# A hybrid decoder trunk in which 17 of 22 FFN column blocks use a seven-product scheme: other buffers, other summing and another order for its weight combinations

## The chip, the cores and the metric

The kernel runs on one core of one Trainium2 chip. Times are device microseconds of one execution; the median of three executions is compared. Matmul operands are fp32 values split in two fp32r parts, a rounded "high" one and the "low" rest, so that each product of a 128x128 weight block with 260 activation columns takes three matmuls (high x high, high x low, low x high).

## The reference, cut to what matters

```
for l in range(2):                                  # 512 prompt tokens and 8 sample tokens
    m = mixer(rmsnorm(h, w_mix_pre))                # gated DeltaNet and retention heads, one input, one output projection
    h = h + rmsnorm(m, w_mix_post)
    x = rmsnorm(h, w_ffn_pre)
    gate, up = split(x @ w_gate_up)                 # 1024 -> 2 x 2816
    h = h + rmsnorm((silu(gate) * up) @ w_down, w_ffn_post)
```

The change is in the product x @ w_gate_up and in silu(gate) * up; everything else is the same in both kernels.

## The kernel before, in words

The activations lie transposed: hT has 8 blocks of 128 model rows, and the 520 tokens as two halves of 260 columns. A layer is a long run of matmuls on TensorE (PE). Weights arrive as 512 KB slabs in two stage buffers (SP issues them, line 481), ScalarE (ACT) rounds each to Wh (line 1313) and VectorE (DVE) takes the rest Wl (line 1865), three slabs deep.

The gate and up matrices have 22 column blocks each. The first NP = 5 pairs are computed directly, as 10 tiles of 48 matmuls (the first three tiles by halves in `first_halves`, line 687, the other seven at line 681). DVE takes gate tile i = 2j out of PSUM (line 2461) and up tile i = 2j+1 (line 2479), each with the norm's factor `rb`; PE's tile i waits until tile i-2 has been taken out. Between these two instructions DVE also runs `x_scaled`, `x_sum` and `x_low`, which make the seven combinations of activations (tile XU), and ACT runs `weighted` (line 1709) and `x_high` for them.

The other Q = 17 pairs q go by a Strassen-Winograd scheme, `strassen(q)` (lines 1234 to 1236): the 2x2 blocks are gate and up (rows) by upper and lower half of the model dimension, and by the two token halves. Seven products UA11, US2, US1, UA12, US3, US4, UA22, in this order, of 12 matmuls each, replace eight. Their weights are quarters of the block column, QW = 512 columns wide each: those of UA11, UA12 and US4 are single quarters; US1 and US3 are sums of two quarters, US2 of three, UA22 of four. The seven outputs go to three PSUM banks (a, b, c), so that US3 and UA22 both accumulate on b after US2. Even and odd q use different banks (4, 5, 6 and 0, 1, 2), and three sets of buffers hold full, high and low weights: C for q = 0, B for odd, A for even q.

What makes the weights of pair q before: SP loads quarter (0,0) twice with one 512 KB transfer (line 503, semaphore b11), quarter (1,1) twice with another (line 508) and quarter (0,1) (line 509). POOL then adds quarter (1,0) to one copy of each by two accumulating DMAs (lines 659 and 663, t1 and t3), which wait for the plain loads. DVE adds US2 (line 2403) and UA22 (line 2412). ACT rounds blocks two by two (`w_high`, line 1732), DVE takes the rests (`w_low`, line 2420). The loads for q go into the set that q-2 used, so line 503 waits until product US1 of q-2 is done, line 508 until US4 is.

What takes the products out: ACT copies the first (`first_copy`, p1, line 1739); DVE runs five `post` instructions per q: U2 (line 2430), TD (2432), C22 (2435), C12 (2437), C21 (2439); ACT does two SiLU halves (lines 1745, 1749); DVE multiplies (`gated`, line 2446). PE's US3 waits for post U2, US4 for TD, UA22 for C22. Each engine runs its list in program order: DVE's order per q is C21 of q-1, the last `w_low` of q, `gated`, then the sums and rests of q+1 between the posts of q. After the 17 pairs comes the down projection (lines 681 and 687), for which the state buffers dst (loaded and stored by POOL) also serve a decode update.

Of the kernel before, what the change touches and what calls it, by code (L numbers as in the profile page):

```python
# [8 lines left out]
def trunk(nc, xT, w_slabs, w_ba, w_rows, dt_bias, a_log, conv_hist, state_gdn, state_ret, c_f32, c_rope,  # L9
# [7 lines left out]
    P = 128  # L17
    KT = 8
# [47 lines left out]
    U2, TD, C22, C12, C21 = range(1, POSTS + 1)  # L66
    P1_COPY, C11_SILU, C21_SILU, HALVES = 1, 2, 3, 3
    W_T2, W_T4, W_LO, W_STEPS = 1, 2, 3, 6
# [30 lines left out]
    with ctx:  # L99
# [142 lines left out]
        tdif = at("tdif", A0, XU_N + (FT - 2) * HF, [P, HC])  # L242
# [13 lines left out]
        pu = at("pu", UP0, 0, [P, 2, HC])  # L256
        p1, u2 = pu[:, 0], pu[:, 1]
# [42 lines left out]
        def acc_banks(q):  # L300
            return (0, 1, 2) if q % 2 else (4, 5, 6)
# [80 lines left out]
        def heads_of(i):  # L382
# [23 lines left out]
            "b11_loaded b2_loaded t1_summed t3_summed p_done post_done ffn_rest ffn_round gate_half "  # L406
# [69 lines left out]
        def _(sp):  # L476
# [14 lines left out]
            def quarters(l, q):  # L491

                N = l * Q + q
                w = w_set(q)[2]
                if q == 0:
                    sp.wait_ge(s["state_stored"], (l + 1) * 32)
                elif q < 3:
                    sp.wait_ge(s["tile_done"], l * TILES + T_DN)
                else:
                    sp.wait_ge(s["p_done"], (N - 2) * UN + US1 + 1)  # L500
                if N:
                    sp.wait_ge(s["b11_loaded"], N * 16)
                sp.dma_start(w[:, UA11:US1 + 1:2], quarter(l, q, 0, 0).unsqueeze(1).to_broadcast([P, 2, QW])).then_inc(s["b11_loaded"], 16)
                if q >= 3:
                    sp.wait_ge(s["p_done"], (N - 2) * UN + US4 + 1)
                if N:
                    sp.wait_ge(s["b2_loaded"], N * 32)
                sp.dma_start(w[:, US3:US4 + 1], quarter(l, q, 1, 1).unsqueeze(1).to_broadcast([P, 2, QW])).then_inc(s["b2_loaded"], 16)
                sp.dma_start(w[:, UA12], quarter(l, q, 0, 1)).then_inc(s["b2_loaded"], 16)
# [65 lines left out]
        def _(pool):  # L575
# [13 lines left out]
            for l in range(DEPTH):  # L589
# [59 lines left out]
                pool.wait_ge(s["dr_mm"], (l + 1) * 16)  # L649
                load_state(l, 0, False)  # L650
                load_state(l, 1, False)
                for q in range(Q):

                    N = l * Q + q
                    w = w_set(q)[2]
                    if N:
                        pool.wait_ge(s["t1_summed"], N * 16)
                    pool.wait_ge(s["b11_loaded"], (N + 1) * 16)
                    pool.dma_start(w[:, US1], quarter(l, q, 1, 0), accum_op=ALU.add).then_inc(s["t1_summed"], 16)
                    if N:  # L660
                        pool.wait_ge(s["t3_summed"], N * 16)
                    pool.wait_ge(s["b2_loaded"], (N + 1) * 32)
                    pool.dma_start(w[:, US3], quarter(l, q, 1, 0), accum_op=ALU.add).then_inc(s["t3_summed"], 16)
# [11 lines left out]
        def _(pe):  # L675
# [53 lines left out]
            for l in range(DEPTH):  # L729
# [474 lines left out]
                def strassen(q):  # L1204
# [3 lines left out]
                    a_, b_, c_ = acc_banks(q)  # L1208
                    for u, bank in enumerate((a_, b_, c_, a_, b_, c_, b_)):
                        if q == 0:  # L1210
                            pe.wait_ge(s["ffn_rest"], l * REST + 8 + u + 1)
                        if u % 2 == 0:
                            pe.wait_ge(s["ffn_rest"], l * REST + X_STEPS + q * W_STEPS + W_LO + u // 2)
                        if u == UA11:
                            if q == 0:
# [6 lines left out]
                        elif u == US2 and q >= 2:  # L1222
                            pe.wait_ge(s["post_done"], (N - 2) * POSTS + C21)
                        elif u == UA12:
                            pe.wait_ge(s["gate_half"], N * HALVES + P1_COPY)
                        elif u == US3:
                            pe.wait_ge(s["post_done"], N * POSTS + U2)
                        elif u == US4:
                            pe.wait_ge(s["post_done"], N * POSTS + TD)
                        elif u == UA22:  # L1230
                            pe.wait_ge(s["post_done"], N * POSTS + C22)
                        for k in range(4):
                            cols = slice(k * P, (k + 1) * P)
                            mm(PS[:, bank, 0:HC], hi_[:, u, cols], XU[:, u, 0, k], start=k == 0 and u < 3, stop=False, skip_group_check=True)  # L1234
# [63 lines left out]
        def _(act):  # L1298
# [16 lines left out]
            for l in range(DEPTH):  # L1315
# [399 lines left out]
                def w_high(q, c):  # L1715
# [3 lines left out]
                    us = slice(2 * c, min(2 * c + 2, UN))  # L1719
                    if c == 0:  # L1720
                        act.wait_ge(s["b11_loaded"], (N + 1) * 16)
                        act.wait_ge(s["ffn_rest"], l * REST + X_STEPS + q * W_STEPS + W_T2)
                    elif c == 1:
                        act.wait_ge(s["t1_summed"], (N + 1) * 16)
                        act.wait_ge(s["b2_loaded"], (N + 1) * 32)
                    elif c == 2:
                        act.wait_ge(s["t3_summed"], (N + 1) * 16)
                    else:
                        act.wait_ge(s["ffn_rest"], l * REST + X_STEPS + q * W_STEPS + W_T4)
                    if q >= 3:  # L1730
                        act.wait_ge(s["p_done"], (N - 2) * UN + us.stop)
# [978 lines left out]
```

## Time and profile before

| what | value |
| --- | --- |
| median of 3 runs | 1453.88 us (1452.79 to 1454.06) |
| the profiled execution's own time | 1450.49 us |
| its span, first to last instruction | 1448.7 us |
| mean granted TensorE clock | 0.988 |
| first layer's seven-product stage | 392.5 to 587.2 us |
| second layer's | 1110.2 to 1305.8 us |

The span is what the trace's rows cover; the profiled execution's own time has 1.8 us more around it. Rows are in microseconds from the span's start. A matmul's row lasts 0.28 us but the next one starts 0.12 us after it, since they overlap: so the time between starts is what counts.

### The profile page before, as it was taken

The numbers are of one execution on the slowest core, as the hardware profiler recorded it, in microseconds if no ns is written. First come the engines' busy times: TensorE is split into PE (matmuls) and PEld (weight loads), VectorE is DVE, ScalarE is ACT, GpSimd is POOL, SyncE is SP. The second block draws the span as 40 slices with busy tenths as digits, with TensorE's granted clock in tenths as the row PEclk, the third lists the DMA queues.
The fourth block names the chain that finished last, engine by engine and source line by source line (L and its number), as shares of the span: only waits on it lengthen the run. The fifth ranks groups of instructions, "written<-read, shape, count | busy, mean of one in ns | idle before, by whom it ended". The sixth has DMA issues, their size and how long they took to land.

```text
span 1448.7 us, 29260 instructions
## 1 busy us (share of the span) xinstructions
PE 1386.1 (96%) x12172; PEld 1354.6 (94%) x12172; DVE 997.2 (69%) x1641; ACT 626.7 (43%) x1196; POOL 159.7 (11%) x209
## 2 busy tenths in 40 slices
PE   9999999998989999999999999999988989999997
PEld 8999999998988989999999999999988889999997
DVE  7745896877666767854586568877766666677544
ACT  5135464465433434522442364643753444354222
POOL 0001211100011111011000011210001111110110
PEclk9999999999999999999999999999999999999998
DMA  5331341131466675355313322421224566653552
GB/s 200 117 102 60 96 131 62 62 105 59 119 144 158 164 162 150 120 178 180 122 59 117 103 68 86 118 75 63 91 90 126 128 159 174 156 140 129 179 183 77
DMA packets 81092, 174.20 MB, mean 120 GB/s; under 512 B 20673, under 2 KB 24129, under 8 KB 80961
## 3 DMA queue, kind: packets, MB, share of 16 engines
q1 hardware_dynamic: 63344, 128.81, 28.1%
q0 software_dynamic: 17616, 43.53, 12.7%
q8 instruction: 96, 1.57, 0.4%
q14 instruction: 36, 0.29, 0.1%
HBM read 159.53 MB, written 12.78 MB: 119 GB/s over the span
## 4 chain that ended last, share of the span: by engine, by line
PE 71%; DMA 12%; DVE 11%; issue 3%; ACT 2%; SPq 1%; DVEq 0%; ACTq 0%; POOLq 0%
PE PS L681 46%; DMA fullB<-w_slabs 8%; PE PS L687 4%; PE PS L1234 4%; PE PS L1236 3%; PE PS L1235 3%; DMA fullA<-w_slabs 3%; DVE loB L2420 1%; DVE Wl L1865 1%; DVE hT L1903 1%; DVE Xl L1882 1%; DVE mT L1902 1%; DVE loA L2420 1%; PE PS L875 1%; DVE conv L1992 1%
## 5 line engine op out<-in xcount | busy, mean ns | idle before, releaser
L681 PE MATMUL PS<-Xh,Wh 128*128 128x260 f32 x1376 | 287.7, 290 | 11.6 <-DVE sqb L2479 9.3
L1313 ACT ACTIVATE Wh<-stage 128x1024 fp32r<-128x1024 f32 x143 | 151.1, 1058 | 339.5 <-PE PS L681 322.6
L681 PE MATMUL PS<-Xh,Wl 128*128 128x260 f32 x1376 | 278.6, 284 | 0.0
L681 PE MATMUL PS<-Xl,Wh 128*128 128x260 f32 x1376 | 278.2, 284 | 0.0
L1865 DVE TENSOR_TENSOR Wl<-stage,Wh 128x1024 fp32r<-128x1024 f32 x143 | 174.6, 1222 | 103.8 <-ACT Wh L1313 103.2
L681 PEld LDWEIGHTS PS<-Xh,Wh 128*128 128x128 f32 x1376 | 213.8, 191 | 15.6 <-issue 11.0
L681 PEld LDWEIGHTS PS<-Xl,Wh 128*128 128x128 f32 x1376 | 213.6, 190 | 0.0
L681 PEld LDWEIGHTS PS<-Xh,Wl 128*128 128x128 f32 x1376 | 213.5, 190 | 0.0
L1234 PE MATMUL PS<-XU,hiA 128*128 128x260 f32 x448 | 128.9, 288 | 14.4 <-DVE pu L2430 7.4
L1234 PE MATMUL PS<-XU,hiB 128*128 128x260 f32 x448 | 128.5, 287 | 10.0 <-DVE pu L2430 4.8
L1236 PE MATMUL PS<-XU,loA 128*128 128x260 f32 x448 | 126.9, 283 | 0.0
L1236 PE MATMUL PS<-XU,loB 128*128 128x260 f32 x448 | 126.9, 283 | 0.0
L1235 PE MATMUL PS<-XU,hiB 128*128 128x260 f32 x448 | 126.5, 282 | 0.0
L1235 PE MATMUL PS<-XU,hiA 128*128 128x260 f32 x448 | 126.5, 282 | 0.0
L681 PE MATMUL PS<-actH,Wh 128*128 128x260 f32 x616 | 124.0, 282 | 0.0
L681 PE MATMUL PS<-actH,Wl 128*128 128x260 f32 x616 | 123.9, 282 | 0.0
L681 PE MATMUL PS<-actL,Wh 128*128 128x260 f32 x616 | 123.9, 282 | 0.0
L1234 PEld LDWEIGHTS PS<-XU,hiA 128*128 128x128 f32 x448 | 84.3, 188 | 18.9 <-DVE fullB L2403 8.4
L681 PEld LDWEIGHTS PS<-actH,Wh 128*128 128x128 f32 x616 | 97.2, 188 | 1.4
L1234 PEld LDWEIGHTS PS<-XU,hiB 128*128 128x128 f32 x448 | 84.3, 188 | 13.5 <-DVE fullA L2403 5.8
L1732 ACT ACTIVATE hiB<-fullB 128x1024 fp32r<-128x1024 f32 x64 | 57.4, 945 | 87.9 <-DMA fullB<-w_slabs 33.2
L681 PEld LDWEIGHTS PS<-actL,Wh 128*128 128x128 f32 x616 | 94.8, 188 | 0.0
(380 smaller groups left out, 2916.5 us busy)
## 6 DMA issues: line engine op xcount, KB each, us to landing
stage<-w_slabs SPq DMA_DIRECT2D x143, 512.0 KB, 3.4
fullB<-w_slabs SPq DMA_DIRECT2D x32, 512.0 KB, 4.5
fullA<-w_slabs SPq DMA_DIRECT2D x32, 512.0 KB, 4.7
dst<-state_ret POOLq DMA_DIRECT2D x32, 256.0 KB, 3.7
dst<-state_gdn POOLq DMA_DIRECT2D x32, 256.0 KB, 4.1
fullB<-w_slabs POOLq DMA_DIRECT2D x32, 256.0 KB, 5.8
fullA<-w_slabs POOLq DMA_DIRECT2D x32, 256.0 KB, 5.1
fullB<-w_slabs SPq DMA_DIRECT2D x16, 256.0 KB, 5.4
```

Source lines behind the costliest of these rows:

```text
L681: ins = mm(pj(slot)[:, a], w[:, ws, pos, :], x[:, a, :], start=first and w is Wh and x is xh, stop=last and w is Wl)
L687: ins = mm(pj(slot)[:, a], w[:, ws, pos, :], x[:, a, :], start=first and w is Wh and x is xh, stop=last and w is Wl)
L875: ins = mm(PS[rows, 7, B_U:B_U + P], vectors, dst[:, u % 2, j, :], start=n == 0, stop=n == 7 and u < 8, skip_group_check=True)
L1234: mm(PS[:, bank, 0:HC], hi_[:, u, cols], XU[:, u, 0, k], start=k == 0 and u < 3, stop=False, skip_group_check=True)
L1235: mm(PS[:, bank, 0:HC], hi_[:, u, cols], XU[:, u, 1, k], start=False, stop=False, skip_group_check=True)
L1236: ins = mm(PS[:, bank, 0:HC], lo_[:, u, cols], XU[:, u, 0, k], start=False, stop=k == 3, skip_group_check=True)
L1313: A(Wh[:, G % NW], stage[:, G % NS], ACT.Copy).then_inc(s["hi_split"], 1)
L1732: A(hi_[:, us], full[:, us], ACT.Copy).then_inc(s["ffn_round"], 1)
L1865: V.tensor_tensor(Wl[:, G % NW], stage[:, G % NS], Wh[:, G % NW].bitcast(fp32), ALU.subtract).then_inc(s["lo_split"], 1)
L1882: V.scalar_tensor_tensor(Xl[:, k, a], hT[:, k, a], prm[:, layer, row:row + 1], Xh[:, k, a].bitcast(fp32), ALU.mult, ALU.subtract).then_inc ...
L1902: step(V.tensor_tensor(src, src, rb[:, a:a + 1].to_broadcast([P, k1 - k0, HC]), ALU.mult))
L2420: V.tensor_tensor(lo_[:, us], full[:, us], plain(hi_[:, us]), ALU.subtract).then_inc(s["ffn_rest"], 1)
```

## The change

Quarter blocks are loaded once each into buffers of their own (raw1 holds two, raw12, raw21) and SP starts the load for the next pair when DVE has read the buffer. POOL adds nothing any more; DVE makes US1 and US3 with one instruction. The seventh product gets a fourth PSUM bank, the fifth is added in place, the third is copied by ACT (m5). The order of work on ACT and DVE is rewritten: DVE makes nearly all weights of q+1 during q, and around the direct tiles ACT's `weighted` and DVE's `x_scaled`, `x_sum` and `x_low` come behind the instructions that empty PSUM. p1 and u2 lie in rb, m5 where tdif was.

```diff
-    U2, TD, C22, C12, C21 = range(1, POSTS + 1)
+    U2, U3, C22, C12, C21 = range(1, POSTS + 1)
@@
+        p1, u2 = rb[:, 0], rb[:, 1]
+        raw1 = at("raw1", RP0, 0, [P, 2, QW])
+        raw12 = at("raw12", UP0, 0, [P, QW])
+        raw21 = at("raw21", W0, 2 * UN * QW, [P, QW])
@@ acc_banks
-            return (0, 1, 2) if q % 2 else (4, 5, 6)
+            return (0, 1, 2, 3) if q % 2 else (4, 5, 6, 7)
@@ quarters (SP)
+                    sp.wait_ge(s["ffn_rest"], used + W_T13)
+                sp.dma_start(raw12[:], quarter(l, q, 1, 0)).then_inc(s["b12_loaded"], 16)
...
+                    sp.wait_ge(s["ffn_rest"], used + W_LO05)
+                sp.dma_start(raw1[:, 0], quarter(l, q, 0, 0)).then_inc(s["b1_loaded"], 16)
+                sp.dma_start(raw1[:, 1], quarter(l, q, 1, 1)).then_inc(s["b1_loaded"], 16)
...
+                    sp.wait_ge(s["ffn_rest"], used + W_LO3)
+                sp.dma_start(raw21[:], quarter(l, q, 0, 1)).then_inc(s["b21_loaded"], 16)
@@ POOL
+                pool.wait_ge(s["ffn_rest"], l * REST + X_STEPS + (Q - 1) * W_STEPS + W_LO05)
                 load_state(l, 0, False)
                 load_state(l, 1, False)
-                for q in range(Q):
...
-                    pool.dma_start(w[:, US1], quarter(l, q, 1, 0), accum_op=ALU.add).then_inc(s["t1_summed"], 16)
...
-                    pool.dma_start(w[:, US3], quarter(l, q, 1, 0), accum_op=ALU.add).then_inc(s["t3_summed"], 16)
@@ strassen (PE)
-                    for u, bank in enumerate((a_, b_, c_, a_, b_, c_, b_)):
+                    for u, bank in enumerate((a_, b_, c_, a_, b_, c_, d_)):
...
+                            pe.wait_ge(s["ffn_rest"], l * REST + X_STEPS + q * W_STEPS + W_LO12)
...
                         elif u == US3:
+                            pe.wait_ge(s["ffn_rest"], l * REST + X_STEPS + q * W_STEPS + W_LO46)
                             pe.wait_ge(s["post_done"], N * POSTS + U2)
                         elif u == US4:
-                            pe.wait_ge(s["post_done"], N * POSTS + TD)
-                        elif u == UA22:
-                            pe.wait_ge(s["post_done"], N * POSTS + C22)
+                            pe.wait_ge(s["gate_half"], N * HALVES + M5_COPY)
+                        elif u == UA22 and q >= 2:
+                            pe.wait_ge(s["post_done"], (N - 2) * POSTS + C21)
@@ ACT
                 for j in range(NP):
...
-                    if j == 0:
-                        for k in range(KT):
-                            weighted(k)
                     act.wait_ge(s["tile_free0"], (T0 + T_GU + 2 * j) // 2 + 1)
                     A(gp, gp, ACT.Silu).then_inc(s["gate_silu"], 1)
                     if 2 * j + 1 + NW < 2 * NP:
                         hi(G0 + S_GU + 2 * j + 1 + NW)
+                    if j < 2:
+                        for k in range(4 * j, 4 * j + 4):
+                            weighted(k)
...
                     if q:
                         gate_second(q - 1)
+                    if q + 1 < Q:
+                        w_high(q + 1, W_HI05)
                     first_copy(q)
                     if q + 1 < Q:
-                        w_high(q + 1, 0)
-                        w_high(q + 1, 1)
+                        w_high(q + 1, W_HI3)
+                        w_high(q + 1, W_HI12)
+                        fifth_copy(q)
+                        w_high(q + 1, W_HI46)
                         gate_first(q)
-                        w_high(q + 1, 2)
-                        w_high(q + 1, 3)
@@ DVE, new and changed steps
+                    V.tensor_tensor(full[:, US1:US3 + 1:2], raw1[:], raw12[:].unsqueeze(1).to_broadcast([P, 2, QW]), ALU.add).then_inc(s["ffn_rest"], 1)
...
+                    V.tensor_tensor(full[:, US2], full[:, US1], raw1[:, 1], ALU.add).then_inc(s["ffn_rest"], 1)
...
+                    elif n == U3:
+                        dve.wait_ge(s["post_done"], N * POSTS + U2)
+                        ins = V.tensor_tensor(p1, PS[:, b_, 0:HC], p1, ALU.add)
                     elif n == C22:
+                        dve.wait_ge(s["gate_half"], N * HALVES + M5_COPY)
+                        dve.wait_ge(s["post_done"], N * POSTS + U3)
+                        ins = V.tensor_tensor(up[:, 1], m5[:], p1, ALU.subtract)
@@ DVE, direct tiles: gate tile taken out, then
-                    if j == 0:
-                        x_scaled(0)
-                    elif j == 1:
+                    if j == 1:
+                        x_scaled(2)
                         x_scaled(3)
-                        x_sum(0)
...
+                    elif j == 4:
+                        w_sums13(0)
                         w_sum2(0)
-                        w_sum4(0)
+                        w_low(0, W_HI05)
@@ up tile taken out, product, then
                     if j == 0:
+                        x_scaled(0)
                         x_scaled(1)
-                        x_scaled(2)
...
+                    elif j == 4:
+                        w_sum4(0)
+                        w_low(0, W_HI3)
+                        w_low(0, W_HI12)
+                        w_low(0, W_HI46)
@@ DVE, the order per q
                     if q:
                         post(q - 1, C21)
+                    if q + 1 < Q:
+                        w_sums13(q + 1)
+                        w_sum2(q + 1)
+                        w_low(q + 1, W_HI05)
+                        if q:
+                            gated(q - 1)
+                        post(q, U2)
+                        w_sum4(q + 1)
+                        w_low(q + 1, W_HI3)
+                        w_low(q + 1, W_HI12)
+                        post(q, U3)
+                        post(q, C22)
+                        w_low(q + 1, W_HI46)
+                        post(q, C12)
```

HI05, HI3, HI12 and HI46 name the products (by their number 0 to 6 in the order above) whose weights one instruction rounds, W_LO05 and so on those whose rest is taken; T13, T2 and T4 are the sums for US1 and US3, for US2 and for UA22.

## Rows read from the trace of the kernel before

**Rows 1.** Stretch: length, busy (count) of PE, PEld, DVE, ACT, POOL, clock, DMA share, GB/s

```profile
392.00:588.00 196.00, 181.34 (x1435) 177.30 (x1436) 135.66 (x206) 81.07 (x121) 27.90 (x32) 0.98 0.64 158
```

**Rows 2.** PE in short stretches: length, busy (count), granted clock, DMA share, GB/s

```profile
347.20:352.20 5.00, 4.99 (x25) 0.55 0.13 32
1065.50:1070.50 5.00, 4.96 (x30) 0.70 0.15 32
392.50:397.50 5.00, 4.99 (x29) 0.66 0.85 273
1110.10:1115.10 5.00, 4.94 (x23) 0.50 0.86 261
605.00:615.00 10.00, 10.00 (x84) 1.00 0.37 133
```

**Rows 3.** Timeline of PE: first seven-product matmul and first down matmul, both layers

```profile
392.51 0.41 PE L1234 MATMUL PS<-XU,hiC 128*128 128x260 f32 x1 [2.71 <-DVE loC L2420]
...
587.17 0.41 PE L681 MATMUL PS<-actH,Wh 128*128 128x260 f32 x2
...
1110.16 0.56 PE L1234 MATMUL PS<-XU,hiC 128*128 128x260 f32 x1 [2.71 <-DVE loC L2420]
...
1305.83 0.41 PE L681 MATMUL PS<-actH,Wh 128*128 128x260 f32 x2
```

**Rows 4.** What ended PE's idle time before line 1234 (us, times)

```profile
  DVE pu L2430: 16.3, 16
...
  DVE sqb L2435: 10.9, 24
```

**Rows 5.** Chain that ended last, within one pair of the first layer

```profile
525.51 3.87 DMA fullB<-w_slabs
...
529.90 6.77 DMA fullB<-w_slabs
```

**Rows 6.** Timeline of DVE in one pair: start, duration

```profile
532.44 1.23 DVE L2420 TENSOR_TENSOR loA<-fullA,hiA 128x1024 fp32r<-128x1024 f32 x1 [1.96 <-ACT hiA L1732]
533.58 0.42 DVE L2437 TENSOR_TENSOR sqb<-PS,pu 128x260 f32<-128x260 f32 x1
...
534.26 0.68 DVE L2420 TENSOR_TENSOR loA<-fullA,hiA 128x512 fp32r<-128x512 f32 x1
534.86 0.69 DVE L2446 TENSOR_TENSOR actF<-sqb 128x520 f32<-128x520 f32 x1
```

**Rows 7.** Timeline of DVE: two sums, the second waiting for the first

```profile
384.69 0.68 DVE L2403 TENSOR_TENSOR fullC<-fullC 128x512 f32<-128x512 f32 x1
385.41 0.69 DVE L2412 TENSOR_TENSOR fullC<-fullC 128x512 f32<-128x512 f32 x1
```

**Rows 8.** DMA issues: KB each, median us from issue to landing

```profile
fullA<-w_slabs SPq DMA_DIRECT2D x16, 256.0 KB, 5.9
...
dst<-state_ret POOLq DMA_DIRECT2D x32, 256.0 KB, 3.7
...
rope<-c_rope SPq DMA_DIRECT2D x1, 520.0 KB, 8.3
```

**Rows 9.** Timelines of PE, ACT and DVE before the fourth direct tile, first layer

```profile
342.27 0.28 PE L687 MATMUL PS<-Xh,Wl 128*128 128x260 f32 x1
347.21 0.77 PE L681 MATMUL PS<-Xh,Wh 128*128 128x260 f32 x2 [4.67 <-DVE sqb L2479]
...
342.60 5.06 ACT L1709 ACTIVATE XF<-hT,prm 128x520 f32<-128x520 f32 x8
347.56 0.62 ACT L1765 ACTIVATE sqb<-sqb 128x520 f32<-128x520 f32 x1
348.09 1.04 ACT L1313 ACTIVATE Wh<-stage 128x1024 fp32r<-128x1024 f32 x1
...
341.32 0.70 DVE L2461 TENSOR_TENSOR sqb<-PS,rb 128x520 f32<-128x520 f32 x1 [0.61 <-ACT rb L1355]
345.21 1.24 DVE L2381 TENSOR_TENSOR XF<-XF,rb 128x1040 f32<-128x1040 f32 x1 [3.20 <-ACT XF L1709]
```

More of the change, by code:

```diff
@@ L1222, in strassen @@
                         elif u == US2 and q >= 2:
-                            pe.wait_ge(s["post_done"], (N - 2) * POSTS + C21)
+                            pe.wait_ge(s["post_done"], (N - 2) * POSTS + U3)
+                        elif u == US1 and q >= 2:
+                            pe.wait_ge(s["post_done"], (N - 2) * POSTS + C12)
                         elif u == UA12:
@@ L1718, in w_high @@
                     lo_, hi_, full = w_set(q)
[L1719 to L1727, printed above, removed]
-                    else:
-                        act.wait_ge(s["ffn_rest"], l * REST + X_STEPS + q * W_STEPS + W_T4)
-                    if q >= 3:
-                        act.wait_ge(s["p_done"], (N - 2) * UN + us.stop)
-                    A(hi_[:, us], full[:, us], ACT.Copy).then_inc(s["ffn_round"], 1)
+                    rest = l * REST + X_STEPS + q * W_STEPS
+                    if c == W_HI05:
+                        act.wait_ge(s["b1_loaded"], (N + 1) * 32)
+                        to, src = hi_[:, UA11:US4 + 1:US4], raw1[:]
+                    elif c == W_HI3:
+                        act.wait_ge(s["b21_loaded"], (N + 1) * 16)
+                        to, src = hi_[:, UA12], raw21[:]
+                    elif c == W_HI12:
+                        act.wait_ge(s["ffn_rest"], rest + W_T2)
+                        to, src = hi_[:, US2:US1 + 1], full[:, US2:US1 + 1]
+                    else:
+                        act.wait_ge(s["ffn_rest"], rest + W_T4)
+                        to, src = hi_[:, US3:UA22 + 1:2], full[:, US3:UA22 + 1:2]
+                    A(to, src, ACT.Copy).then_inc(s["ffn_round"], 1)
                 def first_copy(q):
@@ L2411, in w_sum4 @@
                     dve.wait_ge(s["ffn_rest"], l * REST + X_STEPS + q * W_STEPS + W_T2)
-                    V.tensor_tensor(w[:, UA22], w[:, US2], w[:, UA12], ALU.add).then_inc(s["ffn_rest"], 1)
+                    V.tensor_tensor(full[:, UA22], full[:, US2], raw21[:], ALU.add).then_inc(s["ffn_rest"], 1)
                 def w_low(q, c):
                     lo_, hi_, full = w_set(q)
-                    us = slice(2 * c, min(2 * c + 2, UN))
-                    if c == 0:
+                    if c == W_HI05:
+                        us, src = slice(UA11, US4 + 1, US4), raw1[:]
+                    elif c == W_HI3:
+                        us, src = UA12, raw21[:]
+                    else:
+                        us = slice(US2, US1 + 1) if c == W_HI12 else slice(US3, UA22 + 1, 2)
+                        src = full[:, us]
@@ L2424, in post @@
                     N = l * Q + q
-                    a_, b_, c_ = acc_banks(q)
-                    part = {U2: US2, TD: US1, C22: US3, C12: US4, C21: UA22}[n]
-                    dve.wait_ge(s["p_done"], N * UN + part + 1)
+                    a_, b_, c_, d_ = acc_banks(q)
+                    if n != C22:
+                        dve.wait_ge(s["p_done"], N * UN + {U2: US2, U3: US3, C12: US4, C21: UA22}[n] + 1)
                     if n == U2:
@@ L2508, in _ @@
                         gated(q - 1)
-                    if not last:
-                        w_sum2(q + 1)
-                    else:
                         rest_act(0, 2)
-                    post(q, U2)
-                    if not last:
-                        w_sum4(q + 1)
-                    else:
+                        post(q, U2)
                         rest_act(2, 2)
-                    post(q, TD)
-                    if not last:
-                        w_low(q + 1, 0)
-                        w_low(q + 1, 1)
-                    else:
@@ L2523, in _ @@
                         lo(G0 + S_DN)
                         rest_act(4, 2)
-                    post(q, C22)
-                    if not last:
-                        w_low(q + 1, 2)
-                    else:
+                        post(q, U3)
+                        post(q, C22)
                         rest_act(6, 2)
-                    post(q, C12)
+                        post(q, C12)
                 lo(G0 + S_DN + 1)
```

111 lines of the change are left out of this document (46 added, 65 removed).

## The prediction

> **What bounds the kernel now.** I first read the busy times of the seven-product stretch [rows 1]. PE is busy for 181.34 of 196.00 us, VectorE for 135.66, ScalarE for 81.07. PE is the bound, yet it has holes. In the down projection, without holes and at full clock, 10 us hold 84 matmuls [rows 2], so one matmul costs 0.12 us. A pair q is 7 x 12 = 84 matmuls, 10.08 us, and 17 pairs are 1428 x 0.12 = 171.36 us.
>
> The PE timeline [rows 3] gives what the stage takes: 587.17 - 392.51 = 194.66 us in the first layer and 1305.83 - 1110.16 = 195.67 in the second. The excess is 23.30 and 24.31 us, 47.6 together; one pair takes (194.66 + 195.67) / 34 = 11.48 us, not 10.08.
>
> The waits say who makes the holes [rows 4]: 16.3 us on post U2 (line 2430, before US3) and 10.9 us on post C22 (line 2435, before UA22). VectorE isn't out of time, so something holds it. The chain through one pair [rows 5] names it: a plain load of 3.87 us, then an accumulating one, started from POOL, of 6.77 us. They stand in series, 10.6 us, and VectorE's sums and rests come behind: that loop can't turn in 10.08 us. VectorE's instruction before the posts was itself idle for 1.96 us [rows 6].
>
> A second loss lies ahead of the stage [rows 9]. The third tile's last matmul starts at 342.27, the fourth tile's first at 347.21: 4.94 us instead of 0.12. PE waits for line 2479, which stands behind `x_scaled(0)` (345.21), and that waited 3.20 us for ScalarE's eight `weighted` (342.60, 5.06 us).
>
> **The change, part by part.**
>
> *Direct tiles.* The up tile's evacuation no longer has `x_scaled(0)` ahead of it. The gate tile's starts at 341.32; at the step of 0.61 that such a pair of instructions has (0.70 less 0.09) it starts at 341.93, ends at 342.62, and PE goes on 0.15 later (before: 345.21 + 1.15 + 0.70 + 0.15 = 347.21), at 342.77. The hole falls from 4.94 to 0.50: 4.44 saved per layer, 8.9 in all.
>
> The clock goes with it. After the hole, 5 us hold 25 matmuls in the first layer and 30 in the second, at granted clocks of 0.55 and 0.70, against 41.7 at full clock [rows 2]: 16.7 x 0.12 = 2.0 and 11.7 x 0.12 = 1.4 us, 3.4 in all. A hole of 0.5 us won't do this; those of about 1.3 us within the stage [rows 4] are followed by full pace.
>
> What moved comes back as new waits. ScalarE loads a table until 342.60, SiLU takes 0.53 and a slab's rounding about 1.0 [rows 9]; four `weighted` at 0.63 then end at 346.7. `x_scaled(0)` and `(1)` take 2.3 (1.15 each) and stand ahead of the third tile's gate evacuation, 349.05 to 349.74, so the fifth tile starts at 349.89. PE is done with the fourth at 342.77 + 5.76 = 348.53: a wait of 1.36. The same again: SiLU and a rounding from 349.78, four `weighted` until 353.9, two `x_scaled`, evacuation until 356.9, start at 357.04, while PE was ready at 355.65: 1.39. After these the evacuations come in time. Cost 2.75 per layer, 5.5 in all; the bounds are 0 (if PE's queue covers it) and 4 per layer.
>
> *Handover to the first pair.* Before, PE sat idle for 2.71 us for evacuation, product and one rest [rows 3]. Now `w_sum4` and the short rest of HI3 come in too, 0.60 each [rows 6], before the rest PE waits for: 1.2 more per layer, 2.4 in all. The first loads don't matter: they are issued as soon as the slabs' queue allows, over 15 us ahead, though raw21 has to wait for the eighth direct tile.
>
> *The stage itself.* Time R is a pair's first matmul. I take VectorE's steps from start to start [rows 6]: a two-block instruction 1.14 (533.58 - 532.44), two posts 0.68 (534.26 - 533.58), so 0.34 each, a one-block one 0.60, `gated` 0.61. An instruction that waits for the one before it steps by 0.72 rather than 0.60 [rows 7]. Per pair there are five posts (1.70), three rests of two blocks and `w_sums13` (4.56), `w_sum2`, `w_sum4` and the one-block rest (1.80), `gated` (0.61), and two such waits (0.24): 8.9 us, under 10.08. Added against before is `w_sums13`, 1.14, in place of both POOL sums.
>
> In order: C21 of q-1 starts at R+0.20, `w_sums13` 0.55, `w_sum2` 1.81, a rest 2.43, `gated` 3.58, U2 4.19 (done 4.6), `w_sum4` 4.54, rests 5.14 and 5.74, then U3. PE wants U2 at R+5.76: 1.1 to spare. U3 needs US3, done at about R+7.36, so VectorE waits until 7.40; U3, C22, a rest and C12 end at 9.75. C21 comes at R+10.28: 0.5 to spare. UA22 has a bank of its own and no longer waits for this pair's posts. US4 needs m5, which ScalarE copies at R+4.6, wanted at 7.20. ScalarE has eight instructions, none longer than 1.06: at most 8.5 us. The holes at US3 and UA22 go.
>
> *Loads.* Each is single-buffered, so its loop has to turn within a pair. raw1 is the tightest: `w_sums13`, `w_sum2` and the rest take 1.26 + 0.60 + 1.22 = 3.1, the second issue and semaphores about 0.5, then the landing. A quarter landed in 5.9 us behind a 512 KB transfer and a state block of its size in 3.7 [rows 8]. That makes 7.3 to 9.5, under 10.08; I take the lower half, since each pair loads 1.05 MB instead of 1.8 MB of plain and accumulating traffic (the stretch moved 158 GB/s [rows 1]). POOL's two first state loads now wait for the last pair's raw1; their reader comes in the down projection, ten and more us later: nothing. At the last pair, `fifth_copy` stands ahead of a slab's rounding, 0.4 us with 3 to spare: nothing.
>
> *Left of the excess.* The clock after the handover. The first 5 us held 29 matmuls in the first layer and 23 in the second [rows 2], 12.7 x 0.12 = 1.5 and 18.7 x 0.12 = 2.2. The idle time grows, and the second layer wasn't yet at full clock: I take 2.1 per layer, 4.2, with bounds 3.0 and 7.
>
> **Sum:** -8.9 - 3.4 + 5.5 + 2.4 - 47.6 + 4.2 = -47.8 us. The profiled execution took 1450.49, so 1402.7; the median of the runs is 3.4 us above it, which gives **1406 us**. Bounds of the single terms: -55 (no new waits, short clock losses) to -43 (4 us of waits per layer, 7 of clock), so 1399 to 1411. A measurement of this kernel tells 0.2%, 2.9 us, from nothing.
>
> **The rivals.**
>
> *VectorE becomes the bound.* For: 8.9 us of 10.08 rest on instructions starting up to 0.09 us before the one ahead ends. If thirteen of them with their semaphores each ended first, they would take 9.73 us in full durations plus 13 x 0.04: 10.25 per pair, 0.17 over PE. 34 x 0.17 = 5.8 us, so 1412. Against: the early starts are between instructions that have semaphore waits now [rows 6]. The Trainium skill ("VectorE: DVE Perf Modes", section "The DRAIN you can't avoid") says that the next instruction does not start until the pipeline is empty; by that rule the sum would be this rival's. The row at 533.58 shows a start every 0.34 us for 0.42 us posts, so here the trace bears it out only for dependent ones.
>
> *Loads come late, in part.* The raw1 loop needs a landing under 6.5 us. At 6.9 a pair takes 10.5, 34 x 0.42 = 14 us more: 1420. For: three more loads share SP's queue, each issue holding it; against: less traffic. This also covers the case that the new waits in the direct tiles grow.
>
> *Slower than before.* The place is the same loop, `w_sums13` ahead of all posts: single buffers put load, sums and rest in series, which the old kernel had spread over two sets. From a landing of 8.0 us on, the pair takes over 11.6 us and eats the 4.5 us gained outside. 8.3 us was seen once, for a table load with many others in flight [rows 8]: (3.6 + 8.3 - 11.48) x 34 - 4.5 = +10, 1464. Against it speaks every other row. The Trainium skill ("DMA: Bandwidth & Descriptors", section "Measured (HBM→SBUF, 128 partitions, SWDGE, issued from GpSimd)") tells to batch transfers to at least 1 MiB; its rule speaks against cutting 512 KB transfers into quarters, and by it this loop would be slower than a joint load. The state block's row, a quarter MB in 3.7 us, shows no such penalty.
>
> *It doesn't do what it says:* the posts stay late because ScalarE's rounding of raw1 holds `first_copy`, now behind it. It would move US3's hole to UA12, some 0.5 us a pair: 1423. The order gives 1.9 us to spare.
>
> **How the numbers follow.** My forecast 0.72, VectorE bound 0.12, loads partly late or ScalarE late 0.12 together, slower 0.03, 0.01 for an exact balance. The range takes the forecast's bounds and the second and third case's times: 1400 to 1420. Faster 0.96, same 0.01, slower 0.03.
>
> **What would show it.** Right: the seven-product stage is 173 to 175 us in each layer; no POOL transfers of weights; gaps before US3 and UA22 under 0.1 us; pairs start every 10.1 us; C21 starts 0.2 us after PE ends the pair, with VectorE idle before it. In the direct tiles a hole of 0.5 us before the fourth tile and two new ones of 1.4. Wrong: VectorE never idle and PE waiting for a rest or for U2; `w_sums13` waiting for raw1; landings over 6 us; a hole over 5 us at the handover.

## The result, and the profile after

The changed kernel took 1403.72 us (median of 4 runs, 1401.79 to 1404.53) against 1453.34 us (4 runs): ratio 0.9665, 95% interval 0.9638 to 0.9693. The prediction was 1406. Run again on another occasion it took 1403.68 us, ratio 0.9665 (0.9647 to 0.9683). The profiled execution took 1401.79 us with a span of 1400.0, where the sum had 1402.7 for it. The sum was added up for the profiled execution, and 3.4 us were put on it for the median; in the changed kernel the median lies 1.9 us above the profiled execution.

The two stretches of seven products, and PE in short stretches; columns as in [rows 1] and [rows 2]:

```profile
388.00:561.00 173.00, 172.74 (x1426) 172.77 (x1427) 151.83 (x218) 84.49 (x138) 1.11 (x2) 0.99 0.30 106
1083.00:1256.00 173.00, 172.61 (x1425) 172.64 (x1426) 151.76 (x218) 84.41 (x138) 1.11 (x2) 0.99 0.30 106
```

```profile
341.00:346.00 5.00, 4.90 (x41) 1.00 0.37 125
1036.10:1041.10 5.00, 4.90 (x41) 1.00 0.35 127
388.20:393.20 5.00, 4.94 (x30) 0.69 0.27 102
1083.30:1088.30 5.00, 4.91 (x28) 0.66 0.29 102
```

PE is busy all through the stage, and VectorE for 152 of 173 us where it was 136 of 196 [rows 1]. The DMA engines move 106 GB/s instead of 158. The fourth direct tile starts at full clock (41 matmuls in 5 us where [rows 2] had 25 and 30).

The PE timeline, first layer, first and last matmul of the stage and what is left of the holes around it:

```profile
341.10 0.48 PE L676 MATMUL PS<-Xh,Wh 128*128 128x260 f32 x2 [0.20 <-DVE sqb L2493]
...
348.18 0.36 PE L676 MATMUL PS<-Xh,Wh 128*128 128x260 f32 x1 [1.12 <-DVE sqb L2476]
...
355.32 0.36 PE L676 MATMUL PS<-Xh,Wh 128*128 128x260 f32 x1 [1.17 <-DVE sqb L2493]
...
388.26 0.56 PE L1231 MATMUL PS<-XU,hiC 128*128 128x260 f32 x1 [3.91 <-DVE loC L2433]
...
561.25 0.41 PE L676 MATMUL PS<-actH,Wh 128*128 128x260 f32 x2
...
579.53 0.50 PE L1197 MATMUL PS<-vblk,krows 96*128 96x512 f32 x1 [0.40 <-DVE vblk L2369]
```

The stage takes 561.25 - 388.26 = 172.99 us, in the second layer (1083.39 to 1256.45) 173.06: 44.3 us less than in [rows 3]. What ended PE's idle time before the stage's first lines has one entry left, the start of the stage itself:

```profile
its engine sat idle before it (us, times) until:
  DVE loC L2433: 16.0, 4
```

The four are PE and its weight loads, in both layers; the two entries of [rows 4] are gone. One pair on VectorE, which answers to [rows 6]:

```profile
531.20 0.43 DVE L2454 TENSOR_TENSOR sqb<-PS,rb 128x260 f32<-128x260 f32 x1 [0.44 <-PE PS L1233]
531.54 1.22 DVE L2409 TENSOR_TENSOR fullB<-raw,raw 128x1024 f32<-128x1024 f32 x1
532.79 0.69 DVE L2414 TENSOR_TENSOR fullB<-fullB,raw 128x512 f32<-128x512 f32 x1
...
535.14 0.42 DVE L2443 TENSOR_TENSOR rb<-PS,rb 128x260 f32<-128x260 f32 x1
...
536.69 1.22 DVE L2433 TENSOR_TENSOR loB<-fullB,hiB 128x1024 fp32r<-128x1024 f32 x1
538.40 0.43 DVE L2446 TENSOR_TENSOR rb<-PS,rb 128x260 f32<-128x260 f32 x1 [0.50 <-PE PS L1233]
538.94 0.43 DVE L2450 TENSOR_TENSOR sqb<-m,rb 128x260 f32<-128x260 f32 x1
...
541.28 0.43 DVE L2454 TENSOR_TENSOR sqb<-PS,rb 128x260 f32<-128x260 f32 x1 [0.44 <-PE PS L1233]
```

The pair's matmuls start at R = 531.00. C21 comes at R+0.20, U2 at R+4.14, U3 at R+7.40 after 0.50 us of waiting for PE, and the next C21 10.08 us after the first. VectorE now waits for PE twice a pair, and PE for nobody.

The loads, as in [rows 8]; all four quarters of a pair are in one row:

```profile
raw<-w_slabs SPq DMA_DIRECT2D x136, 256.0 KB, 2.6
```

**Where 48.7 us of span went.** It is read off PE's rows. From the last matmul before the hole to the stage's first, the direct tiles took 392.51 - 342.27 = 50.24 us and take 388.26 - 340.62 = 47.64, and in the second layer 49.54 and 47.68: 4.5 us. The stages give 44.3. What follows a stage got longer, by 1.0 us from the first stage's end to the second layer's hole and by 0.7 us from the second stage's end to the end: 1.7. The last 1.65 us are the start of the program: the last matmul before the first hole starts at 340.62 where it started at 342.27, and the change doesn't touch what is ahead of it. This execution had a granted clock of 1.00 in the span from 3 to 23 us (117 matmuls), the one of before 0.91 (104 matmuls). So 47.0 us are the change's, where the sum had 47.8. The repetition agrees: it had 102 matmuls at 0.91, its last matmul before the hole starts at 342.47, and its span is 46.7 us under that of before.

### The profile page after: what moved, and what is told of

Read it like the earlier page. It is cut to its first block, busy times and chain, and to the rows that moved or that the text cites. A ratio compares the mean times of both kernels' runs of the same rounds, so it can differ in the third digit from the quotient of the medians.

```text
span 1400.0 us, 29086 instructions
## 1 busy us (share of the span) xinstructions
PE 1366.9 (98%) x12172; PEld 1343.3 (96%) x12172; DVE 1040.2 (74%) x1675; ACT 634.9 (45%) x1230; POOL 100.7 (7%) x141
## 4 chain that ended last, share of the span: by engine, by line
PE 83%; DVE 10%; ACT 3%; issue 2%; DMA 1%; SPq 0%; DVEq 0%; ACTq 0%
PE PS L676 43%; PE PS L1231 8%; PE PS L1232 8%; PE PS L1233 8%; PE PS L682 5%; DVE Wl L1873 2%; DVE hT L1911 1%; ACT Wh L1310 1%; DVE Xl L1890 1%; ACT XF L1706 1%; DVE actL L2467 1%; ACT actH L1756 1%; DVE mT L1910 1%; PE PS L870 1%; PE PS L1197 1%
## 5 line engine op out<-in xcount | busy, mean ns | idle before, releaser
L676 PEld LDWEIGHTS PS<-actH,Wl 128*128 128x128 f32 x616 | 94.8, 188 | 0.0
```

The costliest lines, as they stand in the source:

```text
L676: ins = mm(pj(slot)[:, a], w[:, ws, pos, :], x[:, a, :], start=first and w is Wh and x is xh, stop=last and w is Wl)
```

## The experiments

Differences are taken from 1403.7 us, and each ratio is to the kernel before on the run's own occasion. On four occasions the kernel before took 1449.7 to 1453.3 us (medians), so differences between times of two occasions are uncertain by some 3 us. The lengths of the stages are read from the traces, two for each run.

### The transfers that add, taken out of the old kernel

```diff
-                    pool.dma_start(w[:, US1], quarter(l, q, 1, 0), accum_op=ALU.add).then_inc(s["t1_summed"], 16)
...
-                    pool.dma_start(w[:, US3], quarter(l, q, 1, 0), accum_op=ALU.add).then_inc(s["t3_summed"], 16)
@@ ACT and DVE, waits
-                        act.wait_ge(s["t1_summed"], (N + 1) * 16)
+                        act.wait_ge(s["b11_loaded"], (N + 1) * 16)
```

> The kernel before with POOL's two accumulating transfers per pair left out (quarter (1,0) is missing from the weights of US1, US3, US2 and UA22); the instructions that waited for them wait for the plain loads. Everything else is old: order, three banks, buffers. Theory (the serial pair of transfers, 3.9 and 6.8 us, is what holds the old stage): the stage falls from 195 us to about 173 to 178 a layer, 1410 to 1420. Rival (the old order on VectorE and the shared bank make most of the holes): the stage stays over 185 us, 1430 and up.

1409.83 us, ratio 0.9712 (0.9697 to 0.9726). The stage takes 174.08 and 175.33 us. Its first matmul and the first of the down projection, and PE's idle time before the stage's first line:

```profile
393.68 0.55 PE L1222 MATMUL PS<-XU,hiC 128*128 128x260 f32 x1 [2.71 <-DVE loC L2408]
...
567.76 0.41 PE L669 MATMUL PS<-actH,Wh 128*128 128x260 f32 x2
```

```profile
  DVE loC L2408: 11.2, 4
  issue: 1.3, 3
  DVE sqb L2423: 0.7, 2
```

With the old order, three banks and two buffer sets, the stage is within 1.1 and 2.3 us of the changed kernel's as soon as nobody waits for an addition by a transfer. So the accumulating transfers were the cause: 20.6 and 20.3 us of the 23.3 and 24.3. The waits in [rows 4] on posts were their effects, passed on by VectorE's list. This run takes away the wait and the traffic together: the DMA engines move 128 GB/s in the stage instead of 158, and the joint 512 KB loads land in 3.9 and 4.0 us (medians) instead of 4.7 and 4.5. How much of the gain is the lighter traffic isn't told apart, but the 0.5 to 0.8 us at the landings are small beside the accumulating transfer's 6.77 in [rows 5].

Which loop was too long can be read from the kernel before. The 3.87 and 6.77 us of [rows 5] don't come back to their own start within one pair: with two buffer sets the load of a pair waits for product US1 of two pairs earlier. One turn for set B, SP's issues and the matmul that waited in between:

```profile
525.51 0.37 SPq L503 DMA_DIRECT2D fullB<-w_slabs  x1
...
548.28 0.37 SPq L503 DMA_DIRECT2D fullB<-w_slabs  x1
```

```profile
538.60 0.36 PE L1234 MATMUL PS<-XU,hiA 128*128 128x260 f32 x1 [0.48 <-DVE pu L2430]
```

From the issue to US3's first matmul (load, addition, VectorE's US2 sum, which stands ahead of post U2) it is 13.09 us. From there to the end of US1 of the next pair, which frees the set, PE has 72 matmuls, 8.64 us. That makes 21.7 us for two pairs, for which PE alone needs 20.16; with the hole before UA22 the turn took 22.8. Without the accumulating transfer's 6.77 us it has room, as this run shows.

The kernel leaves out one quarter of the weights; putting it back costs VectorE 1.14 us a pair, and whether the old order has room for that was not tried.

### The seventh product back in bank b

```diff
-                    for u, bank in enumerate((a_, b_, c_, a_, b_, c_, d_)):
+                    for u, bank in enumerate((a_, b_, c_, a_, b_, c_, b_)):
...
+                        elif u == UA22:
+                            pe.wait_ge(s["post_done"], N * POSTS + U3)
```

> The changed kernel with the seventh product back in bank b, so that UA22 of a pair waits until U3 of the same pair has read it. Theory (VectorE reads U3 on time now, at R+7.4 to 7.8, before UA22 wants the bank at R+8.64; the bank as such is worth nothing): 1403.7 within 2, stage 173 us. Rival (the fourth bank is what took the holes before UA22 away): 0.6 us a pair, 34 x 0.6 = +20, about 1424.

1402.02 us (1400.56 to 1403.29), ratio 0.9676 (0.9656 to 0.9695), beside 0.9665 for the changed kernel; the stage takes 173.62 and 173.58. U3 is read in time here too:

```profile
540.20 0.43 DVE L2446 TENSOR_TENSOR rb<-PS,rb 128x260 f32<-128x260 f32 x1 [0.50 <-PE PS L1233]
```

The stages are 0.6 and 0.5 us longer than the changed kernel's 172.99 and 173.06, the time isn't. The fourth bank is worth nothing that can be measured. The holes before UA22 went because U3 (and C22, which it took the bank from) come on time. Only in the last pair, where U3 stands behind a rest, PE waits 0.25 us for it, in both layers.

### The old order around the direct tiles

```diff
+                    if j == 0:
+                        for k in range(KT):
+                            weighted(k)
                     act.wait_ge(s["tile_free0"], (T0 + T_GU + 2 * j) // 2 + 1)
                     A(gp, gp, ACT.Silu).then_inc(s["gate_silu"], 1)
...
+                    if j == 0:
+                        x_scaled(0)
                     done(t + 1)
                     freed(V.tensor_tensor(up, pj(1), rb[:], ALU.mult), t + 1)
```

> The changed kernel with the old order around the ten direct tiles (all eight weighted before the first SiLU, x_scaled(0) ahead of the first up tile's evacuation, and so on); the seven-product part stays new. Theory (the new order there is worth what the prediction summed): a hole of 4.7 to 4.9 us and its slow clock come back before the fourth direct tile, the two waits of 1.3 us go, 4.4 + 1.7 - 2.6 = 3.5 us per layer, +7 us against the changed kernel: about 1410.5. The stage of the seven products stays at 173 us. Rival (the activations' order is hidden or gives back all it takes): within 2 us of 1403.7.

1412.41 us, ratio 0.9747 (0.9727 to 0.9766): 8.7 us above the changed kernel by the times, 12 by the ratios, expected 7. The hole before the fourth tile is back (4.67 us idle), the two waits are gone, and 5 us hold 25 matmuls again in the first layer and 23 in the second. The way from the hole to the stage is 3.7 and 4.0 us longer, as expected within 0.5. The stage too takes 174.14 and 174.32, 1.2 us more, and that sits in its first 5 us:

```profile
393.00:398.00 5.00, 4.98 (x23) 0.50 0.30 98
1092.30:1097.30 5.00, 4.94 (x23) 0.50 0.33 105
```

The idle time before it is the same 3.91 us as in the changed kernel, and still 23 matmuls got through instead of 30 and 28. That needn't be the old order's doing. The changed kernel's own repetition has the same 3.91 us, 29 matmuls behind it in the first layer and 22 in the second:

```profile
1084.30:1089.30 5.00, 4.90 (x22) 0.50 0.32 106
```

Its stages take 173.04 and 174.04 us. So 7.7 us are shown to be the old order's. The other 2.4, of the two stages, aren't: the changed kernel's own second stage differs by 1.0 from one execution to the next.

### VectorE's spare time: one and two more instructions per pair

```diff
+                    for _ in range(again):          # 1 or 2, for the rest of HI05 alone
+                        step(V.tensor_tensor(lo_[:, us], src, plain(hi_[:, us]), ALU.subtract))
```

> The changed kernel with one more 128x1024 instruction on VectorE per pair (the rest of HI05 taken once more into the same place), ahead of post U2; it steps by 1.26 us. Theory (VectorE needs 8.9 of 10.08 us per pair): U2 comes at about R+5.8 instead of 4.6 where PE wants it at 5.76, so 0.1 to 0.2 us a pair, +3 to +7 us: 1407 to 1411. Rival (VectorE needs 9.7 or more): 0.9 us a pair and more, +29, 1430 and up.

1412.58 us, ratio 0.9725 (0.9709 to 0.9741), +8.9: over the theory's 7, far under the rival's 29. With one more instruction PE waits for U2, and VectorE for PE only 0.16 us a pair. Rows of VectorE (the pair from `w_sums13` to `w_sums13`) and of PE (the pair's first matmul and US3's first):

```profile
487.33 0.42 DVE L2454 TENSOR_TENSOR sqb<-PS,rb 128x260 f32<-128x260 f32 x1
487.83 0.43 DVE L2456 TENSOR_TENSOR sqb<-PS,rb 128x260 f32<-128x260 f32 x1
488.18 1.22 DVE L2409 TENSOR_TENSOR fullA<-raw,raw 128x1024 f32<-128x1024 f32 x1
...
493.04 0.42 DVE L2445 TENSOR_TENSOR rb<-PS,rb 128x260 f32<-128x260 f32 x1
...
498.58 1.22 DVE L2409 TENSOR_TENSOR fullB<-raw,raw 128x1024 f32<-128x1024 f32 x1
```

```profile
487.63 0.29 PE L1231 MATMUL PS<-XU,hiB 128*128 128x260 f32 x1
...
493.61 0.36 PE L1231 MATMUL PS<-XU,hiB 128*128 128x260 f32 x1
```

The pair takes 10.40 us, 0.32 more than 10.08, with an instruction more that steps by 1.25. So U2 had 0.93 us to spare in the changed kernel (the prediction had 1.1). The loop goes through both engines: C21 (487.83) waits for PE's end of the pair, VectorE's list leads to U2 (493.04), PE's US3 waits for U2 (493.61), and PE ends the pair. C21 needs nothing of the post ahead of it, yet it steps by 0.50 instead of 0.34, and it starts 0.20 us after the next pair's first matmul as in the changed kernel: those 0.16 us are a wait for PE. VectorE's own list is therefore 10.40 - 1.25 - 0.16 = 8.99 us in the changed kernel, against 8.9 predicted and 9.7 in the rival.

> The same with two more such instructions, 2.52 us. Theory: VectorE is now the bound, 8.9 + 2.5 = 11.4 us a pair, 1.4 us over the changed kernel's on 32 pairs: +43, about 1447, back at the kernel before. Rival (9.7 or more of work): 12.2 us a pair, +68, 1470.

1450.92 us, ratio 1.0001 (0.9992 to 1.001): expected 1447. Pairs take 11.57 and 11.62 us on average, those in the middle 11.66 (US3's first matmul at 432.69 and 444.35), 1.26 more than with one added instruction. PE now waits 1.3 us a pair for U2. Two superfluous instructions a pair eat up the whole gain.

### raw1 loaded 3.3 us later in each pair

```diff
-                    sp.wait_ge(s["ffn_rest"], used + W_LO05)
+                    sp.wait_ge(s["ffn_rest"], used + W_LO12)
                 sp.dma_start(raw1[:, 0], quarter(l, q, 0, 0)).then_inc(s["b1_loaded"], 16)
```

> The changed kernel with the two raw1 loads issued 3.3 us later in each pair, after the rest of HI12 instead of the rest of HI05. Theory (a quarter lands in 2.6 us, so the loop of 6.4 + 0.5 + 2.6 = 9.5 us still turns within a pair): within 2 us of 1403.7. Rival (the loads land close to when VectorE wants them, as the 5.9 us of the old rows would have it: 12.8 us a pair): +85, about 1489.

1415.49 us, ratio 0.9753 (0.9738 to 0.9767), +11.8: neither case. One turn of the loop, SP's issues and VectorE's first sum:

```profile
491.76 0.33 SPq L508 DMA_DIRECT2D raw<-w_slabs  x1
492.13 0.43 SPq L509 DMA_DIRECT2D raw<-w_slabs  x1
```

```profile
485.37 1.22 DVE L2409 TENSOR_TENSOR fullA<-raw,raw 128x1024 f32<-128x1024 f32 x1 [1.09 <-DMA raw<-w_slabs]
...
495.77 1.23 DVE L2409 TENSOR_TENSOR fullB<-raw,raw 128x1024 f32<-128x1024 f32 x1 [1.18 <-DMA raw<-w_slabs]
```

The loop turns in 10.40 us: 6.39 from the sum to the issue, 0.37 to the second issue, then 3.64 from there to the sum. Three loads now go out within 0.9 us and their median landing is 3.4 us, not 2.6. So this loop is real, and the theory missed by its landing. In the changed kernel the second issue comes 3.47 us after the sum (535.01 after 531.54), and with a landing of 2.6 us the loop needs some 6.3 us of 10.08, an estimate from these rows.

### The handover and the direct tiles, repaired

The first run moves `w_sum4` and two rests of the first pair ahead of the last up tile's evacuation, and lets PE start with the rest of HI05 alone:

```diff
+                        if u == US2:
+                            pe.wait_ge(s["ffn_rest"], l * REST + X_STEPS + q * W_STEPS + W_LO12)
                         if u == UA11:
-                            pe.wait_ge(s["ffn_rest"], l * REST + X_STEPS + q * W_STEPS + W_LO12)
+                            pe.wait_ge(s["ffn_rest"], l * REST + X_STEPS + q * W_STEPS + W_LO05)
...
                         w_low(0, W_HI05)
+                        w_sum4(0)
+                        w_low(0, W_HI3)
+                        w_low(0, W_HI12)
                     done(t + 1)
```

> The changed kernel with w_sum4, the rest of HI3 and the rest of HI12 of the first pair put ahead of the last up tile's evacuation, and PE's wait for the rest of HI12 moved from the first product to the second. Theory (the 3.9 us hole at the handover is VectorE's order alone, and the slow clock behind it is the hole's): hole under 0.5 us, no slow clock, (3.7 + 1.6) x 2 = -10.6, about 1393. Rival (the clock falls in any case when the first pair starts, or PE waits at the second product instead): half of it or less, 1398 and up.

1391.52 us, ratio 0.9604 (0.9584 to 0.9623), -12.2. There is no hole and no slow clock, in the second layer (44 matmuls at 1.00) as in the first:

```profile
385.60:390.60 5.00, 5.00 (x44) 1.00 0.35 119
```

The stage takes 172.22 and 172.21 us, with 0.67 us of waiting for U2 of the first pair, which is late next. So its slow start was the hole's. The rows give 4.0 us for the hole and 0.8 for the stage in each layer, 9.7 in all; the other 2.5 of the 12.2 are within what two occasions differ by.

The second moves `x_scaled`, `x_sum` and the first `x_low` one evacuation on:

```diff
                     if j == 1:
-                        x_scaled(2)
-                        x_scaled(3)
+                        x_scaled(0)
+                        x_scaled(1)
...
```

> The run with the early rests, and besides x_scaled, x_sum and the first x_low each one evacuation later (x_scaled(0) and (1) behind the third tile's gate evacuation instead of ahead of it). Theory (the two waits of 1.3 us in the direct tiles are x_scaled standing ahead of an evacuation): both go, -2.6 per layer, -5 in all: about 1388. Rival (the later activations delay the weights of the first pair, and the handover's hole comes back): no gain over the other run or a loss, 1393 and up.

1390.27 us, ratio 0.9592 (0.957 to 0.9614), within the noise of the run before. Both waits of 1.3 us are gone, but the first pair now has two, 0.52 before the rest of US2's weights and 1.41 before U2 (was 0.67), and the stage takes 173.6 instead of 172.2: 2.6 gained and 1.35 given back, with this the rival's case by half.

The third adds a change in the down projection: the rest of one slab's weights goes behind the first value block on VectorE, which PE waited for in the run before.

> The run with early rests and later activations, and besides, in the down projection's fifth slab step, VectorE copies the decode rows out of PSUM and makes the first value block before it takes that slab's rest instead of after. Theory (PE's new wait of 0.56 us for the value block is VectorE's list, which since the change has one more post in its full last stretch): the wait goes, -0.6 to -0.7 us per layer, the stages stay at 173.6: 1 us under the run before, about 1389. Rival (the slab's rest is then late and PE waits for it): the same or slower.

```diff
-                    lo(G0 + S_DN + i + NW)
+                    if i != 1:
+                        lo(G0 + S_DN + i + NW)
...
                     if 1 <= i < 17:
                         value_block(i - 1)
+                    if i == 1:
+                        lo(G0 + S_DN + i + NW)
```

1388.44 us, ratio 0.9566 (0.9548 to 0.9584), within the noise of the run before. PE's wait for vblk, 0.54 and 0.55 us in the run before, is gone in both layers, the stage is the same (173.55 and 173.61).

The fourth goes after what the second gave back: U2 of the first pair is posted ahead of the next pair's rest of HI05, and the rest of HI12 comes ahead of the rest of HI3, so that US2's weights are ready sooner.

> All of that, and post U2 of the first pair ahead of the second pair's rest of HI05, and the first pair's rest of HI12 ahead of the rest of HI3. Theory: the first pair's two holes of 0.52 and 1.41 us shrink by 0.5 and 1.1, and what slow clock stands behind them: the stage falls from 173.6 to about 172, -3 us: about 1386. Rival: the holes move to the next product, 1389.

```diff
+                        if q == 0:
+                            post(q, U2)
                         w_low(q + 1, W_HI05)
                         if q:
                             gated(q - 1)
-                        post(q, U2)
+                            post(q, U2)
```

1387.96 us, ratio 0.956 (0.9542 to 0.9577). The stage falls to 172.56 and 173.16 us, but the first pair has two small waits in the first layer (0.57 and 0.23 us) and three in the second (0.34, 0.45 and 0.52): the rival's case for the most part, and no measurable gain over the run before. It is 4.4% faster than the kernel before, and 15.7 us faster than the changed one.

### The changed kernel once more

> The changed kernel once more, on the same chip and beside the same runs: within 2 us of 1403.7.

1403.68 us (5 runs, 1401.78 to 1404.23), ratio 0.9665 (0.9647 to 0.9683).

## Why the prediction was right, point by point

- **What bounds it.** Right in the cause, wrong in the period. The accumulating transfers made the holes, as the run without them shows. But "that loop can't turn in 10.08" sets 10.6 us of transfers against one pair, and the loop with two buffer sets spans two pairs: 21.7 us and more against 20.16. So 10.6 being above 10.08 shows nothing. Nothing in the sum hung on it either, since the excess was taken from PE's rows. The sum for the stage, -47.6 + 4.2 = -43.4, measured -44.3, in the repetition -43.25.
- **The hole before the fourth tile.** Predicted 4.94 to 0.50, measured 0.48 (341.10 - 340.62); the slow clock behind it is gone in both layers.
- **The new waits in the direct tiles.** Predicted 1.36 and 1.39, measured 1.27 and 1.33 beyond the normal step, in the second layer 1.28 and 1.29. The second layer repeats them, and the run with x_scaled moved takes both away.
- **Handover.** Predicted 1.2 more than 2.71, measured 3.91. The excess of the stage, put at 2.1 a layer for the clock, measured 1.6 and 1.7, in the repetition 1.7 and 2.7.
- **Activations' order as a part.** The sum had -8.9 - 3.4 + 5.5 = -6.8, and with the handover's 2.4 -4.4; the rows gave -4.5 (2.60 and 1.86). Undone by itself the order cost 7.7 us ahead of the stages.
- **VectorE.** Predicted 8.9 us a pair, measured 8.99: the sum had two waits on the instruction ahead at 0.12 us each, and the rows have 0.11 (1.25 instead of 1.14 after `w_sums13`) and 0.18 to 0.20 (0.52 to 0.54 instead of 0.34 after U3). The rival with 10.25 fell with the run of one more instruction. In the changed kernel too an instruction that needs nothing of the one ahead starts before that one's end in the records: after C21 of 0.43 us the next starts 0.34 us later (531.20 to 531.54), while a dependent one comes 0.54 us after 0.43 (538.40 to 538.94). The Trainium skill ("VectorE: DVE Perf Modes", section "The DRAIN you can't avoid") says that the next instruction waits for an empty pipeline, and adds that one that is not "held" (its word for an instruction that must wait for all before it) starts earlier. The prediction used the first half alone; the second half agrees with the 0.34 us.
- **Loads.** Predicted landings of 3.7 to 5.9, measured 2.6: a mis-sized term, without effect, because the loop had room either way. The rival that ends slower had its breaking point at 8.0 us. The late loads show that this loop is real: 3.3 us later it already costs 0.3 us a pair. The Trainium skill ("DMA: Bandwidth & Descriptors", section "Measured (HBM→SBUF, 128 partitions, SWDGE, issued from GpSimd)") tells to batch to 1 MiB, for 75% of peak bandwidth. The prediction inferred from it that quarters would make this loop slower than a joint load. That doesn't follow: the rule is on bandwidth, beside a table of loads issued from GpSimd, and the loop hangs on the landing time. Here quarters of 256 KB landed in 2.6 us and the joint loads of 512 KB before in 4.5 and 4.7.
- **The banks.** The text said that UA22's own bank frees it from this pair's posts. True, but it is not what removed the holes: without it the time is the same.
- **The term that was put at nothing.** "At the last pair, `fifth_copy` stands ahead of a slab's rounding, 0.4 us with 3 to spare: nothing." The last pair was not free: PE now waits 0.56 us in each layer for the first value block of the down projection, where it didn't wait before. At R+8.6, where C22 alone stood (TD had come earlier, at 582.40, R+5.9), U3 and C22 now stand, the second waiting for the first:

```profile
559.74 0.42 DVE L2446 TENSOR_TENSOR rb<-PS,rb 128x260 f32<-128x260 f32 x1
560.27 0.43 DVE L2450 TENSOR_TENSOR sqb<-m,rb 128x260 f32<-128x260 f32 x1
...
564.39 0.42 DVE L2454 TENSOR_TENSOR sqb<-PS,rb 128x260 f32<-128x260 f32 x1
566.33 1.24 DVE L2467 TENSOR_TENSOR actL<-actF,actH 128x1040 fp32r<-128x1040 f32 x1 [1.52 <-ACT actH L1756]
...
578.79 0.69 DVE L2369 TENSOR_TENSOR vblk<-vrows,cf 96x512 fp32r<-96x512 f32 x1
```

With R = 551.17 the value block starts at R+27.62; in the kernel before, with R = 576.50, at 603.59, R+27.09. VectorE does wait in between, 1.52 us for ScalarE in both kernels, but ScalarE works there behind C21, which is itself 0.5 us later, so the delay goes through. That is one half. The other is PE's: its last pair took 10.67 us before and takes 10.08 now, so it reaches the value block 0.59 us sooner after R. Counted from the down projection's first matmul the block starts at 17.54 us instead of 16.42, and PE wants it done by 17.7 in both. The run that puts the block ahead of a slab's rest took the wait away; the two halves are read from the rows and weren't run apart. The sum had none of this; what follows the stages cost 1.7 us in all.
- **What was luck.** The sum for the profiled execution came out 0.9 us too high. This execution's fast start gave 1.65 us and the loss behind the stages took 1.7, and neither was in the sum; they cancel.

## What to carry to other kernels

A wait's name in the profile is that of the last link: two posts stood in the waits, and the cause was two transfers in series two engines away. Follow the chain until it comes back to its own start, and compare the turn with what the bound engine needs for as many pairs as the turn spans: here 21.7 us and more against 20.16 for two pairs, since there were two buffer sets. With one buffer the turn has to fit into one pair. When everything is then on time, look at the seams (the last direct tile, the first and the last pair): reordering the first pair's weights alone gave 10 to 12 us more, a fifth to a quarter of what the change gave. And when the bound engine gets faster, look again at everything that it reaches sooner.

## What the runs showed that was not expected

- The same idle time of 3.91 us before the stage was followed by 28 to 30 matmuls in 5 us (granted clock 0.66 to 0.69) in some stages and by 22 or 23 (0.50) in others, also in two executions of the same code. A difference of 1 us in one stage says nothing of an edit by itself.
- The span from 3 to 23 us of the program holds 102, 104 or 117 matmuls at granted clocks of 0.91, 0.91 and 1.00 in executions whose code there is the same. It moved the last matmul before the first hole by 1.7 to 1.9 us.
- An accumulating load of a quarter takes 5.1 to 5.8 us at the median to land where plain quarters in their own buffers land in 2.6. The plain ones of before took 5.4 and 5.9 behind a 512 KB one, and 4.3 to 4.4 there without the accumulating loads.
